# Attention product: 64 value columns of the unit's own key head instead of 128

## The reference, cut to what matters

```python
def gqa_attend(qb, k, v):
    s = jnp.einsum('bqhgd,bkhd->bhgqk', qb, k, preferred_element_type=jnp.float32) * HEAD_DIM ** -0.5
    p = jax.nn.softmax(s, axis=-1)
    return jnp.einsum('bhgqk,bkhd->bqhgd', p.astype(v.dtype), v)
```

## Time and profile before

| | |
|---|---|
| runs, median of 3 | 4188.84 us (4185.81 to 4190.89) |
| the profiled execution | 4184.54 us, span 4182.7 us |
| mean granted clock of TensorE | 0.917 of full |
| busy share of the span | PE 86%, PEld 72%, DVE 54%, ACT 30%, POOL 28% |
| attention stage of layer 0 | about 482 to 635 us |
| attention stage of layer 1 | about 1704 to 1830 us |

### The profile page before, as it was taken

One profiled execution on the slowest core, in us unless ns is written; L12 is line 12 of the kernel. 1 busy time (PEld: TensorE's weight loads), 2 busy tenths in 40 slices (PEclk: granted clock), 3 DMA queues, 4 the chain that ended last, 5 costly groups with the idle time before them and its releaser, 6 DMA issues. The chain is left out here.

```text
span 4182.7 us, 56917 instructions
## 1 busy us (share of the span) xinstructions
PE 3584.2 (86%) x22004; PEld 2999.0 (72%) x22004; DVE 2271.7 (54%) x3290; ACT 1249.8 (30%) x1868; POOL 1160.9 (28%) x564
## 2 busy tenths in 40 slices
PE   6955697899998965798997899888988986887998
PEld 4745576788887745677885788767777775775886
DVE  4658562655655347545445588723666766336334
ACT  4113322221222113323223345432333432323222
POOL 4205002232222203014442333143231230423442
PEclk7977898999999977899998999999999998998998
DMA  4420001223222420013331121121111110212221
GB/s 162 166 79 1 1 1 61 76 96 111 107 85 88 166 79 1 1 41 116 116 115 54 66 70 65 46 91 61 46 42 36 46 37 11 96 65 71 96 95 60
DMA packets 85333, 295.30 MB, mean 71 GB/s; under 512 B 13507, under 2 KB 14083, under 8 KB 84741
## 3 DMA queue, kind: packets, MB, share of 16 engines
q1 hardware_dynamic: 84836, 290.74, 19.7%
q10 hardware_dynamic: 288, 1.60, 0.1%
HBM read 290.21 MB, written 2.10 MB: 70 GB/s over the span
## 5 line engine op out<-in xcount | busy, mean ns | idle before, releaser
L222 POOL TENSOR_TENSOR slab_lo<-slab,slab_hi 128x1024 fp32r<-128x1024 f32 x330 | 823.8, 2502 | 2273.1 <-ACT slab_hi L205 2273.1
L205 ACT ACTIVATE slab_hi<-slab 128x1024 fp32r<-128x1024 f32 x330 | 346.2, 1056 | 792.7 <-PE banks L121 473.7
L119 PE MATMUL banks<-hT_hi,slab_hi 128*128 128x512 f32 (+1 forms) x896 | 354.7, 396 | 44.7 <-POOL slab_lo L222 34.3
L120 PE MATMUL banks<-hT_lo,slab_hi 128*128 128x512 f32 (+1 forms) x896 | 349.5, 390 | 0.0
L121 PE MATMUL banks<-hT_hi,slab_lo 128*128 128x512 f32 (+1 forms) x896 | 349.0, 389 | 0.0
L119 PE MATMUL banks<-mlp_hid_hi,slab_hi 128*128 128x512 f32 (+1 forms) x768 | 282.0, 367 | 10.1 <-DVE mlp_hid_lo L1794 10.1
L1794 DVE TENSOR_TENSOR mlp_hid_lo<-mlp_sq,mlp_hid_hi 128x512 fp32r<-128x512 f32 (+1 forms) x96 | 216.6, 2257 | 120.9 <-ACT mlp_hid_hi L1752 120.5
L120 PE MATMUL banks<-mlp_hid_lo,slab_hi 128*128 128x512 f32 (+1 forms) x768 | 279.6, 364 | 0.0
L121 PE MATMUL banks<-mlp_hid_hi,slab_lo 128*128 128x512 f32 (+1 forms) x768 | 279.4, 364 | 0.0
L119 PE MATMUL banks<-slab_hi,hT_hi 128*128 128x256 f32 (+1 forms) x728 | 246.4, 338 | 2.5 <-ACT rT L872 2.5
L119 PEld LDWEIGHTS banks<-hT_hi,slab_hi 128*128 128x128 f32 x896 | 172.4, 192 | 82.1 <-POOL slab_lo L222 35.7
(11 more groups left out here) (552 smaller groups left out, 8251.7 us busy)
## 6 DMA issues: line engine op xcount, KB each, us to landing
slab<-in_s_mlp_dram SPq DMA_DIRECT2D x192, 512.0 KB, 3.6
proj_vec_slab<-in_s_vec_proj_dram SPq DMA_DIRECT2D x64, 512.0 KB, 3.6
mlp_vec_slab<-in_s_vec_mlp_dram SPq DMA_DIRECT2D x64, 512.0 KB, 3.5
slab<-in_s_ssm_dram SPq DMA_DIRECT2D x48, 512.0 KB, 3.5
slab<-in_s_gdn_dram SPq DMA_DIRECT2D x48, 512.0 KB, 3.5
slab<-in_s_in_dram SPq DMA_DIRECT2D x32, 512.0 KB, 4.6
slab<-in_s_out_dram SPq DMA_DIRECT2D x24, 512.0 KB, 3.7
slab<-in_s_merge_ssm_dram SPq DMA_DIRECT2D x24, 512.0 KB, 3.5
```

What stands on the lines that cost most here:

```text
L119: nc.tensor.matmul(out, lhs.hi, rhs.hi, start=start, stop=False)
L120: nc.tensor.matmul(out, lhs.hi, rhs.lo, start=False, stop=False)
L205: self.nc.scalar.activation(hi, self.raw[s][:], ACT.Copy).then_inc(self.rounded, 1)
L222: self.nc.gpsimd.tensor_tensor(pair.lo[:], self.raw[u % slots][:], pair.hi[:].bitcast(F32), ALU.subtract).then_inc(self.split, 1)
```

## The change

The matmul of L1390 streams the 64 value columns of the unit's own key head instead of all 128, and writes 64 output columns at column 256 of the bank instead of 128. `unit_out` reads these 64 columns, where it picked the right half before. Number and order of the instructions on every engine, semaphores and waits stay as they are; the stationary operand `pT` stays 128x128.

```diff
--- before.py
+++ after.py
@@ -1312,10 +1312,9 @@
         def unit_out(dve, n):
 
             h, t = units[n]
-            col = 256 + HD * (h // 4)
             dve.wait_ge(inverted, n + 2)
             dve.wait_ge(o_full, n + 2)
-            nc.vector.tensor_scalar(c.tok[:, t, C_AQ + h * HD:C_AQ + (h + 1) * HD], c.ps[:, 5 + 2 * (n % 2), col:col + HD],
+            nc.vector.tensor_scalar(c.tok[:, t, C_AQ + h * HD:C_AQ + (h + 1) * HD], c.ps[:, 5 + 2 * (n % 2), 256:256 + HD],
                                     sm[:, 3, n:n + 1], None, ALU.mult).then_inc(o_read, 1)
 
         with st.block() as block:
@@ -1387,8 +1386,8 @@
                     h, t = units[n]
                     pe.wait_ge(pT_ready, n + 2)
                     for s in range(keys(t)):
-                        last = nc.tensor.matmul(c.ps[:, 5 + 2 * (n % 2), 256:256 + P], pT[:, n % 2, s * P:(s + 1) * P],
-                                                c.tok[:, s, C_AV:C_AV + P], start=s == 0, stop=s == keys(t) - 1)
+                        last = nc.tensor.matmul(c.ps[:, 5 + 2 * (n % 2), 256:256 + HD], pT[:, n % 2, s * P:(s + 1) * P],
+                                                c.tok[:, s, C_AV + HD * (h // 4):C_AV + HD * (h // 4) + HD], start=s == 0, stop=s == keys(t) - 1)
                     last.then_inc(o_full, 1)
 
                 scores(0)
```

## The result

The changed kernel takes 4396.65 us (4 runs, 4391.92 to 4400.88) against 4187.33 us (4 runs, 4185.38 to 4190.89) in the same session: ratio 1.0494, 95% interval 1.0472 to 1.0516. It is 209 us slower, where 4 us faster was forecast. The profiled execution took 4397.96 us with a span of 4396.1; the mean granted clock of TensorE fell from 0.917 to 0.869.

The account below looks back on a forecast made before the run. TensorE was taken to bound the latent units (119.43 of 122 us busy, clock 1.00); gains of 3.4 (latent) + 0.4 (context) + 0.1 (clock) = 3.9 us off the 4188.84 us median gave 4184.9 us, range 4177 to 4194.

Parts of the forecast that it names:

- Inside a run of products: Product's twelve records: weight load sets the 0.111 us pitch, so halving the columns gains nothing there.
- The boundary: From last product record to next scores: gap falls from 0.205 to 0.15 us, 0.053 per latent unit, 3.4 us in all.
- Context units: 16 units of 1.44 us, one product per two-unit loop: 0.027 us saved each, 0.4 us in all.
- the rivals: Columns set the pitch (4146 us, 0.04); no gain at the boundary (4188.8 us, 0.12); clock falls (4248 us, 0.06).
- The clock as a term of the sum: Start of layer 1: two units at 1.2 GHz save 0.107 us each instead of 0.053, adding 0.1 us.
- The falling clock as a rival: Attention stages: less streaming lowers TensorE's clock; at GLA's 42% share of 1.2 GHz, 63 us more, 4248 us; chance 0.06.
- The sentence of the Trainium skill: TensorE clock: a monitor sets it by recent busyness; the prediction said that by it this change pushes the wrong way.

Follow-up runs that it names:

- late64: Kernel before, with 64 product columns only from the seventh latent unit of each layer on, 128 before that; 4185.85 us against 4186.35, ratio 0.9999.
- fillall64: Changed kernel (64 columns in all units) plus unused products filling TensorE's first wait in both layers, three and five; 4181.64 us against 4188.01 for the kernel before.
- context64: Kernel before, with 64 product columns in the 16 context units only, 128 in the latent units; 4208.16 us, ratio 1.0049.
- cols96: Kernel before, with the product streaming 96 columns instead of 128 in all units; 4208.81 us, ratio 1.0053.
- burst: Changed kernel plus 16 unused 512-column products in each layer, 24 units before the end of its units; 4281.07 us, ratio 1.023 to the kernel before.
- latent64: Kernel before, with 64 product columns in the latent units only, 128 in the context units; 4281.62 us against 4186.35, ratio 1.022.
- fillgap: Kernel before with 64 columns in latent units only, plus five unused 256-column products in layer 1's first wait; 4178.33 us against 4184.99, ratio 0.9985.
- fill128: Kernel before, 128 columns in all units, plus five unused products in layer 1's first wait only; 4183.96 us against 4188.01, ratio 0.9984.
- swapped: Changed kernel with product operands exchanged: 64 value columns stationary, 128 columns moving, output not the reference's; 4194.19 us against 4184.99 for the kernel before, ratio 1.0028.

## Why the prediction was wrong, step by step

- **Inside a run of products: right.** The pitch did not fall with the columns. In late64 twelve records take 1.45 us, and the 0.05 less is the last record's.
- **The boundary: right, 0.053 forecast, 0.05 measured** (1.43 to 1.38 us from the first product record to the scores), and with it the latent unit of 3.58 us (1741.76 - 1738.19 = 3.57 in late64).
- **Context units: right at 2.4 GHz, but the 0.4 us of gain never came into play.** In fillall64 two of them take (499.30 - 496.48)/2 = 1.41 us, as forecast. In the changed kernel they run at 1.2 GHz: there the unit costs 2.52 instead of 1.44 us, and the rivals had priced latent units alone.
- **The clock as a term of the sum: this step failed.** I booked the units of layer 1 that run at 1.2 GHz as "two such units" and a gain of 0.1 us. I took for granted that the clock comes back after them, since it did before. It came back because of the 128 columns, and the change removed just these. In place of a gain of 3.9 us, the clock cost 115 us in layer 0 and 95 in layer 1. The last sign of being wrong that the prediction names, a granted clock of the latent units below 1.00, is the one that came (0.50). The rows were there: the earlier trace rows have a product that starts at 1.2 GHz, where 12 records take 2.77 us (context64, at 539.32), and is over in 2.17, so the clock rose while its columns streamed.
- **The falling clock as a rival: right mechanism, wrong size and chance.** The price per unit was right (6.87 us forecast, 6.78 measured). The share of time at 1.2 GHz was taken from GLA as 42%, for 63 us; it was nearly all of both stages. In the profile layer 0 lost 115 us (483.8 to 748.8 us, 265.0 instead of 150.2) and layer 1 95 us (1819.4 to 2044.0, 224.6 instead of 129.7), 210 in sum. And the 0.06 rested on "TensorE has loads or matmuls under way in the same share of the time as now". That is true, and it does not matter: the busy share after the change is 100% at half the clock. The profile's busy time can't show the missing columns, since a record of the product lasts 0.222 us at 2.4 GHz and the next starts 0.11 after it, so that records overlap with 64 columns as with 128. Cols96 differs from the changed kernel in the columns alone and is as busy, and its latent units are back at 2.4 GHz after one product.
- **The sentence of the Trainium skill** ("TensorE: Matmul & The Clock Gate", "What's actually happening") that a monitor sets the clock by how busy TensorE has lately been stood in the prediction as speaking against the change, and I gave it too little weight. The traces agree with its direction: the product streams half the columns, and the granted clock of the latent units is 0.50 instead of 1.00.

What is shown: the loss is the clock (same instructions at either clock in burst and latent64), 64-column units hold 2.4 GHz where they find it and do not lift the clock to it (latent64, burst), and with the short wait at the start of a layer filled they find it (fillgap, fillall64). What stays open: what besides the wait and the columns decides whether layer 0 falls, since with 128 columns it happened in some executions and not in others.

## What to carry to other kernels

Before narrowing a matmul whose pitch the weight load sets, ask not only what it saves (nothing in the run, half a record at its end) but whether its columns keep or restore TensorE's clock: look in the trace for a place where the clock falls and see which instructions are running when it comes back. A busy share of 100% is no sign that the clock will be granted. Where TensorE waits as here, 1.3 or 2.25 us, at the start of a long dense stage, a few unused matmuls in the wait are worth trying: here 10 records made 102 us of difference with 64 columns, and fillgap is the fastest kernel of this study, 0.15% (0.06 to 0.24%) under the one before.

## What the runs showed of the hardware

- The clock has memory. In one execution (latent64) the latent units of 64 columns ran at 2.4 GHz in all of layer 0 (1.00 from 560 to 630 us) and at 1.2 GHz in layer 1 from the transposes behind the first wait on (0.50 from 1735 to 1835 us).
- The clock fell behind waits of TensorE of 1.29 us (layer 0, with 128 columns in a few executions only) and 2.25 us (layer 1), and with these waits filled it did not (fillgap, fillall64).
- Latent units lifted the clock with 128 and with 96 moving columns, and didn't with 64; context units did not lift it with 64 (context64), with 96 (cols96) or, in fill128's profiled execution, with 128. A run of 32 records of 512 columns lifted it too (burst).
- A change of the weights' shape costs TensorE about 0.1 us: swapped has one more of them per unit than before, at the same number of moving columns, and its unit takes 3.75 us (1733.36 - 1729.61) against 3.63. Over the 80 units that is most of swapped's 9.2 us above the kernel before.
